# Attention turns of a two-block transformer kernel: where ScalarE rounds and VectorE splits weight panels

## The reference

```python
px = split_cols(hx @ w_in)
ya, yca = global_gqa(px[0], px[1], px[2], ...)            # mixer A, 8 heads, 2 kv heads
yb, ycb = neighbourhood_attn(px[3], px[4], px[5], ...)     # mixer B, 8 heads
yc_, ycc = window_gqa(px[6], px[7], px[8], ...)            # mixer C, 8 heads, 2 kv heads
ux = jnp.concatenate([ya, yb, yc_], axis=-1) * jax.nn.silu(px[9])
x = x + gate[:, None, :] * (ux @ w_out)
```

```python
x = x + 0.5 * _swiglu(_rms(x, ffn1_norm[l]), ffn1_wg[l], ffn1_wu[l], ffn1_wd[l])
h = _rms(x, mix_norm[l])
y_a = _nsa(q_a, g_a, kc, vc, ks_, vs_, kw, vw, ...) @ w_branch_nsa[l]
y_b = _moba(q_b, k_b, v_b) @ w_branch_moba[l]
merged = jax.nn.sigmoid(gate_a) * y_a + jax.nn.sigmoid(gate_b) * y_b     # gate_a, gate_b: columns of h @ w_in
x = x + merged @ w_out[l]
x = x + 0.5 * _swiglu(_rms(x, ffn2_norm[l]), ffn2_wg[l], ffn2_wu[l], ffn2_wd[l])
```

## Time and profile before

| | before |
|---|---|
| median of three runs | 1904.51 us (1901.29 to 1907.36) |
| profiled execution | 1903.97 us, span 1902.2 us |
| mean granted clock of TensorE | 0.996 |
| TensorE, weight loads | 1857.3 us (98%), 1608.5 us (85%) |
| VectorE, ScalarE, GpSimd | 1285.2 us (68%), 1084.8 us (57%), 95.3 us (5%) |
| splits L1436 | x468, 577.8 us |
| rounds L911 | x468, 484.3 us |
| weight loads of 1 MB by SyncE | x252, 4.8 us to land |

### The profile page before, as it was taken

The page is one execution under the profiler, slowest core; times in us unless marked ns, Lnnn a source line. Parts: engine busy times, 40 slices in busy tenths (PEclk is TensorE's granted clock), DMA queues, the critical chain, the costliest instruction groups (busy, mean ns, idle before and its releaser), DMA issues.

```text
span 1902.2 us, 33268 instructions
## 1 busy us (share of the span) xinstructions
PE 1857.3 (98%) x12844; PEld 1608.5 (85%) x12844; DVE 1285.2 (68%) x2138; ACT 1084.8 (57%) x1899; POOL 95.3 (5%) x82
## 2 busy tenths in 40 slices
PE   7999999999999999999999999999999999999998
PEld 5878878878788987888889988889888889998887
DVE  6663364477736578775677687767776677687765
ACT  5372264375725477774555567755774555567762
POOL 0000000004000006000000010001000000010001
PEclk9999999999999999999999999999999999999999
DMA  9232242232224223555532355554554642355553
GB/s 349 88 112 89 89 159 109 89 134 89 90 89 152 93 79 133 188 187 186 216 133 90 134 177 194 181 199 177 180 195 177 224 155 90 115 177 191 182 178 132
DMA packets 42501, 285.30 MB, mean 150 GB/s; under 512 B 4928, under 2 KB 6336, under 8 KB 9360
## 3 DMA queue, kind: packets, MB, share of 16 engines
q1 hardware_dynamic: 40832, 278.24, 40.7%
q0 software_dynamic: 1552, 5.42, 0.9%
HBM read 282.59 MB, written 1.05 MB: 149 GB/s over the span
## 4 chain that ended last, share of the span: by engine, by line
issue 49%; PE 41%; DVE 4%; POOL 3%; ACT 2%; DMA 1%; SPq 0%; POOLq 0%; DVEq 0%; ACTq 0%
PE bank L2184 7%; PE bank L2186 7%; PE bank L2185 7%; PE bank L2190 6%; PE bank L2191 3%; PE bank L2425 3%; PE bank L2395 2%; PE bank L2370 2%; POOL work L837 1%; DVE panels_lo L1436 1%; PE bank L2286 1%; DMA token_major<-weights 1%; POOL xT L880 1%; ACT work L1044 1%; ACT panels_hi L911 1%
## 5 line engine op out<-in xcount | busy, mean ns | idle before, releaser
L2190 PE MATMUL bank<-acts,panels_hi 128*128 128x512 f32 x2032 | 717.2, 398 | 4.5 <-DVE xT L1922 2.6
L1436 DVE TENSOR_TENSOR panels_lo<-raw_panels,panels_hi 128x1024 fp32r<-128x1024 f32 x468 | 577.8, 1252 | 187.5 <-ACT panels_hi L911 185.7
L911 ACT ACTIVATE panels_hi<-raw_panels 128x1024 fp32r<-128x1024 f32 x468 | 484.3, 1054 | 253.3 <-PE bank L2186 149.8
L2191 PE MATMUL bank<-acts,panels_lo 128*128 128x256 f32 x2032 | 570.5, 281 | 0.0
L2190 PEld LDWEIGHTS bank<-acts,panels_hi 128*128 128x128 f32 x2032 | 381.5, 188 | 97.8 <-DVE xT L1922 2.8
L2191 PEld LDWEIGHTS bank<-acts,panels_lo 128*128 128x128 f32 x2032 | 384.0, 189 | 0.2
L2184 PE MATMUL bank<-acts,panels_hi 128*128 128x256 f32 (+1 forms) x1112 | 349.6, 314 | 2.9 <-ACT gates L1388 1.2
L2185 PE MATMUL bank<-acts,panels_hi 128*128 128x256 f32 (+1 forms) x1112 | 344.4, 310 | 0.0
L2186 PE MATMUL bank<-acts,panels_lo 128*128 128x256 f32 (+1 forms) x1112 | 344.4, 310 | 0.0
L2184 PEld LDWEIGHTS bank<-acts,panels_hi 128*128 128x128 f32 x1112 | 211.6, 190 | 19.7 <-issue 4.1
L2186 PEld LDWEIGHTS bank<-acts,panels_lo 128*128 128x128 f32 x1112 | 211.7, 190 | 11.1
(11 more groups left out here) (276 smaller groups left out, 1927.0 us busy)
## 6 DMA issues: line engine op xcount, KB each, us to landing
raw_panels<-weights SPq DMA_DIRECT2D x252, 1024.0 KB, 4.8
token_major<-weights SPq DMA_DIRECT2D x4, 1024.0 KB, 9.3
near_bias<-rpb POOLq DMA_DIRECT2D x16, 256.0 KB, 3.5
xT<-xin SPq DMA_DIRECT2D x4, 512.0 KB, 5.9
gates<-weights SPq DMA_DIRECT2D x2, 1024.0 KB, 10.2
near_bias<-weights SPq DMA_DIRECT2D x4, 512.0 KB, 7.2
token_major<-weights SPq DMA_DIRECT2D x2, 512.0 KB, 12.5
out<-xT SPq DMA_DIRECT2D x4, 256.0 KB, 2.4
```

Of the source, the lines that this page charges most:

```text
L911: act.activation(slot_hi(n, a, b), raw_of(n, a, b), ACT.Copy).then_inc(hi_ready, 1)
L1436: dve.tensor_tensor(slot_lo(n, a, b), raw_of(n, a, b), slot_hi(n, a, b).bitcast(F32), ALU.subtract).then_inc(lo_ready, 1)
L2190: pe.matmul(bank.rearrange("p (c t) -> p c t", c=2), whi_, with_rest(xhi_), start=start, stop=False, skip_group_check=True)
L2191: return pe.matmul(bank[:, 0:T], wlo_, xhi_, start=False, stop=stop, skip_group_check=True)
```

## The change

On ScalarE the rounds of a panel half move from behind the exponentials of a turn to behind the copy of the next turn, ahead of its exponentials. So a high half of a head output and a copy pass them. On VectorE the splits move from the end of a turn to right behind the head output of the next turn, ahead of normalization, merge scaling and maxima. The loops get a turn more for it. The halves of the gate panel in block 1 move likewise on both engines, and on VectorE those of panel 1 in block 2.

```diff
@@ ScalarE, attention @@
-            for i in range(len(steps) + 5):
+            for i in range(len(steps) + 6):
...
                     o.then_inc(probT_out, 1)
+                if blk == 1 and 3 <= i < 5:
+                    round_half(ONE["gate" + mixer, st.layer].at["panels"] + 3, i - 3)
+                for r, slot in enumerate(ADA_SLOTS[mixer] if st.panels and blk == 1 else ()):
+                    if 0 <= i - slot - 4 < 2:
+                        round_half(st.at["panels"] + r + 2, i - slot - 4)
+                for r, slot in enumerate(GATE_SLOTS if blk == 2 else ()):
+                    if 0 <= i - slot - 2 < 2:
+                        round_half(st.at["panels"] + r + 2, i - slot - 2)
                 if i < len(steps):
...
                         x.then_inc(exped, 1)
-                if blk == 1 and 2 <= i < 4:
-                    round_half(ONE["gate" + mixer, st.layer].at["panels"] + 3, i - 2)
-                for r, slot in enumerate(ADA_SLOTS[mixer] if st.panels and blk == 1 else ()):
-                    if 0 <= i - slot - 3 < 2:
-                        round_half(st.at["panels"] + r + 2, i - slot - 3)
-                for r, slot in enumerate(GATE_SLOTS if blk == 2 else ()):
-                    if 0 <= i - slot - 1 < 2:
-                        round_half(st.at["panels"] + r + 2, i - slot - 1)
                 j = i - 4
@@ VectorE, attention @@
-            for i in range(len(steps) + 6):
+            for i in range(len(steps) + 7):
...
                     m.then_inc(omul, 1)
+                if blk == 1 and 4 <= i < 6:
+                    split_half(ONE["gate" + mixer, st.layer].at["panels"] + 3, i - 4)
+                if blk == 2 and 1 <= i < 3:
+                    split_half(st.at["panels"] + 1, i - 1)
+                for r, slot in enumerate(ADA_SLOTS[mixer] if st.panels and blk == 1 else ()):
+                    if 0 <= i - slot - 5 < 2:
+                        split_half(st.at["panels"] + r + 2, i - slot - 5)
+                for r, slot in enumerate(GATE_SLOTS if blk == 2 else ()):
+                    if 0 <= i - slot - 3 < 2:
+                        split_half(st.at["panels"] + r + 2, i - slot - 3)
                 j = i - 1
...
                                       ALU.subtract).then_inc(usplit, 1)
-                if blk == 1 and 3 <= i < 5:
-                    split_half(ONE["gate" + mixer, st.layer].at["panels"] + 3, i - 3)
-                if blk == 2 and i < 2:
-                    split_half(st.at["panels"] + 1, i)
-                for r, slot in enumerate(ADA_SLOTS[mixer] if st.panels and blk == 1 else ()):
-                    if 0 <= i - slot - 4 < 2:
-                        split_half(st.at["panels"] + r + 2, i - slot - 4)
-                for r, slot in enumerate(GATE_SLOTS if blk == 2 else ()):
-                    if 0 <= i - slot - 2 < 2:
-                        split_half(st.at["panels"] + r + 2, i - slot - 2)
```

## The result

| | before | changed |
|---|---|---|
| median of 17 runs each | 1902.26 us (1897.99 to 1907.36) | 1908.53 us (1903.5 to 1912.22) |
| profiled execution, span | 1903.97 us, 1902.2 us | 1905.62 us, 1903.8 us |
| mean granted clock there | 0.996 | 0.995 |

The ratio of the times is 1.0028, interval 1.002 to 1.0037: by it the changed kernel is 5.3 us slower (3.8 to 7.0); the two medians themselves lie 6.3 us apart. The forecast was 3.7 us slower than before.

What follows compares the result with a forecast made beforehand. TensorE, busy 98% of the span, was taken as the bound. From 1903.97 us, block 1's gains of 4.4 us and block 2's losses of 8.1 us (4.05 us a layer) gave 1907.7 us, range 1900 to 1913 us.

Steps and rivals of the forecast that it cites:

- product 6, half 1 late: Block 2, each layer: VectorE splits this panel half only after the head output, so TensorE waits 0.8 us.
- product 7, bank late: Block 2, each layer: a split now precedes the merge scaling that frees the product's bank; it starts 0.6 us later.
- product 7, half 1 late: Block 2, each layer: the second half's split ends after the next head output; TensorE waits another 0.75 us.
- merge, half 0 late: Block 2, each layer: first merge panel's split falls behind the last head output; first branch product waits 2.25 us.
- given back at the second branch: Block 2's merge: second branch, which began after a 0.33 us wait, starts only 1.9 us later despite the 2.25 us wait.
- clock: Rival (a), 0.23: the clock falls behind block 2's new merge wait, 1.6 us in each layer, giving 1910.9 us.
- layer 0, mixer A: Block 1: of 2.07 us of waits only 0.3 us (ends 0 and 2.1) won, as ScalarE is nearly always busy.
- layer 0, mixer B: Block 1: earlier copy wins 0.94 us and a 0.38 us head output wait goes; 1.3 us gained.
- layer 1, mixer B: Block 1: the 1.91 us head output wait falls to 0.8 us, the clock may stay up; 1.3 us gained (0 to 2.8).
- layer 1, mixers A and C: Block 1: two short waits each at most, 0.9 us left in all; 0.3 us gained together.
- Rival (b): Block 2's late splits stay hidden because VectorE runs ahead, only the gains reach TensorE: 1899.6 us; chance 0.14.
- rival (c): Whole kernel: the change moves no wait, copies being late for another reason and stage ends having slack: 1904 us; chance 0.08.

Runs made afterwards that it cites:

- the splits alone: VectorE's splits moved in both blocks as in the changed kernel, ScalarE in the order of the kernel before; 1910.53 us, ratio 1.004 to before.
- block 1 alone: Rounds and splits moved only in the mixers of block 1, block 2 in the order of the kernel before; 1897.99 us, ratio 0.9973 to before.
- panels 6 and 7 back: Changed kernel, but panels 6 and 7 of block 2's attention stage split at their old place; 1899.3 us, ratio 0.9996 to before.
- product 6 back: Changed kernel, but panel 6 of block 2's attention stage split at its old place; ran once, trace only, 3.40 and 4.91 us lost in the two layers.
- product 7 back: Changed kernel, but panel 7 of block 2's attention stage split at its old place; ran once, trace only, 4.19 and 4.21 us lost in the layers.
- block 2 alone: Rounds and splits moved only in block 2, block 1 in the order of the kernel before; 1911.0 us, ratio 1.0046 to before.
- the rounds alone: ScalarE's rounds moved in both blocks as in the changed kernel, VectorE in the order of before; 1909.18 us, ratio 1.003 to before.
- the late merge with block 1's old order: Block 1 as before; block 2's rounds moved, and its splits except panels 6 and 7; ran once, trace only, 2.21 and 2.22 us lost.

## Why the prediction held, step by step

**The sum in block 2.** Taken from the same matmul, in the changed kernel's first layer, and priced apart by the experiments:

| step | predicted | measured |
|---|---|---|
| product 6, half 1 late | 0.8 | 0.65 |
| product 7, bank late | 0.6 | 0.56 |
| product 7, half 1 late | 0.75 | 1.02 |
| merge, half 0 late | 2.25 | 2.2 to 2.3 |
| given back at the second branch | -0.35 | -0.6 |
| clock | 0 (a rival) | 1.5 |
| a layer | 4.05 | 5.4 |

Without the clock the rows give 3.9 us against 4.05. The give-back is larger than I wrote, since the old wait of 0.33 us cost more than its length: the two matmuls around it start 0.61 us apart, where 0.12 us is usual. The forecast held the moved rounds in block 2 for free. In the changed kernel they are: with the splits alone the same three steps measure 0.65, 0.57 and 1.0 us. The 0.54 us of the rounds show only where the splits keep their old place.

**The clock.** The forecast had no fall at the merge and called it a rival at 23%, with the price of 1.6 us a layer. It came in both layers, at 1.5 us each. The prediction argued from one wait's length: 1.91 us brought a fall, 2.59 us did not the earlier trace rows. The runs show that length alone is no guide here: a wait of 2.2 us with no late split ahead of it left the clock up four times, and with late splits ahead of it the clock fell nine times of ten. Nor does the 2.6 us wait at 720.88 us, the argument against the rival, always leave the clock up: it fell there in four of the twelve traces (block 1 alone, panels 6 and 7 back, product 6 back, product 7 back), all with block 1's new order, at a cost of up to 0.8 us. The Trainium skill, page "TensorE: Matmul & The Clock Gate", section "A second HAM failure mode: psum-queue depth-cycling", names frequent short idles as a cause of the swinging. With that rule these traces agree in part: without the short waits no fall came at the merge, but short waits alone brought none there either.

**The gains in block 1.** Predicted 4.4 us, measured 6.5 us in the profiled pair.

| | predicted | measured |
|---|---|---|
| layer 0, mixer A | 0.3 | 0.66 |
| layer 0, mixer B | 1.3 | 1.59 |
| layer 0, mixer C | 1.2 | 1.46 |
| layer 1, mixer B | 1.3 | 1.83 |
| layer 1, mixers A and C | 0.3 | 0.71 and 0.26 |

Layer 0 brought 3.7 us against 2.8 us, with no fall of the clock near it in either kernel.

At layer 1's mixer B I took 1.3 us of 0 to 2.8 us. The waits themselves gave little: the kernel with block 2 alone has the old wait, 1.90 us, but no fall, and TensorE gains 1.4 us there all the same, so of the 1.83 us some 1.4 us are the clock's and 0.4 us are left for the shorter wait. Most of the 1.1 us by which that wait is shorter came back, and not as the wait for maxima that I had named: the next head output of this mixer waited, which it hadn't before:

```profile
617.40 0.33 PE L2418 MATMUL bank<-consts_sb,token_major 128*128 128x128 f32 x1 [0.76 <-DVE work L1611]
```

VectorE's old order had the clock's fall near 617 us in three traces of four (that of before, that of the rounds alone, and that of the late merge with block 1's old order; not that of block 2 alone), and the new order in none of eight. So the fall goes with the long wait, but not in each execution.

The 0.71 us at layer 1's mixer A is not shown to be a gain of the change: block 2 alone, with block 1's old order, shows 0.73 us there as well. A fall of the clock near 498 us is mixed up in it, behind a wait of 1.8 us that all traces have; five of twelve have the fall, the two of the main pair among them. Where it is absent, TensorE gains 1.41 us in this mixer with the old order (late merge alone) and 1.9 to 2.0 us with the new one (five traces; 1.7 us with the splits alone). So about 1.4 us is that fall's price, and up to 0.5 us can be the change's where the clock stays up.

**What held as argued.** Layer 0's mixer A kept most of its loss, as ScalarE is full there: of 2.1 us of waits for the copy and the head output 1.4 us are left, 1.2 us of them in one wait, and ScalarE is busy 10.00 us of the 10 us from 124 us on. The raw slots' later loads cost nothing that shows: TensorE's waits list no new cause but splits and the merge scaling. Rival (b), that the late splits would be hidden, and rival (c), that nothing moves, are refuted by every kernel that has block 2's late splits.

So that the forecast came out 0.8 us from the measured median is luck in part. Two errors of opposite sign nearly met: 2.7 us more lost at the merges, which is the clock's, and 2 us more won in block 1, partly the clock's. And the forecast started from one execution of 1903.97 us, 1.7 us above the median of before, which hid most of what the change itself cost beyond the forecast. What stands on its own is the ratio, 1.0028 (1.002 to 1.0037), against a forecast of 1.0019: the sign and the waits were right, and the loss was forecast somewhat too small.

## What to carry to other kernels

A piece of background work can be moved behind the foreground work only where its reader has slack: the same two moves were worth 5 us where the panels had turns to spare, and cost 9 us where the reader stood right behind. Check the last turn of a pipeline by itself, since there the next foreground operation waits for the engine that the background work is meant to feed. Look at producer and consumer of a panel separately: in block 1 moving the splits alone won 5.45 us, moving the rounds alone lost 5.4 us, since splits at their old place then stood waiting for the rounds, and moving both won 6.5 to 7.6 us.

## What the runs showed of the hardware

**A pace of the feed-forward stages that changes by 2% with no cause in the program.** Windows of 100 us in the up projection, the first line of each kernel from block 2's first layer, the second from its second: TensorE is fully busy at a clock of 1.00 in all four, with the same instructions. The kernel before:

```profile
1150.00:1250.00 100.00, 100.00 (x579) 88.22 (x578) 79.04 (x109) 73.59 (x109) 0.00 (x0) 1.00 0.54 189
1720.00:1820.00 100.00, 100.00 (x569) 86.76 (x568) 77.16 (x107) 72.19 (x107) 0.00 (x0) 1.00 0.51 182
```

The changed kernel:

```profile
1150.00:1250.00 100.00, 100.00 (x568) 86.68 (x567) 78.47 (x108) 71.33 (x105) 0.00 (x0) 1.00 0.52 188
1720.00:1820.00 100.00, 100.00 (x579) 87.44 (x578) 78.72 (x109) 73.32 (x108) 0.00 (x0) 1.00 0.53 189
```

579 or 568 matmuls: two paces, a whole stage long, 3.2 us apart there, in either kernel and in either layer. Block 2's first feed-forward stage has them too: from 770 to 870 us it is 568 matmuls before and 579 in the changed kernel, which is the step of -2.65 us. Of twelve traces four have the slow pace at 1150 us (568 matmuls): two of them with a fall of the clock at the merge ahead and two without, three with block 1's new order and one with the old, so it follows neither. What sets it stays open. It is as large as the effect that was to be measured, and is the reason to compare the same matmul inside a stage, and medians for the whole.

**The clock falls with the history, not with one wait,** as above. Two more falls follow no wait at all. Behind 24 matmuls of only 32 columns (968.39 to 970.98 us before, TensorE always busy) the clock fell in nine of the twelve traces, and behind the same 24 in the second layer, near 1552 us, in eight; each cost 1.6 us, whichever order the kernel had. One to five falls stand in a trace, the one at its very end left out. That they differ between executions in places that no edit touched accounts for part of the spread of about 9 us between runs of one kernel.
